# A four-layer fp32 block on one core: split weights kept in place, loads by piece, x turned by the host, two steps moved to ScalarE

## The reference, cut to what matters

```python
def first_block(x, ...):
    x = x + even_layer(x, ...)   # layer 0: chunk attention + mLSTM
    x = x + odd_layer(x, ...)    # layer 1: RG-LRU + gated delta rule
def second_block(x, ...):
    h = _layer_ab(h, ...)        # layer 2: dilated + differential attention
    h = _layer_c(h, ...)         # layer 3: causal attention, 16 heads
    return _rmsnorm(h, final_norm)

def odd_layer(x, ...):
    proj = rmsnorm(x, norm_g) @ w_in
    ...
    qkv = silu(causal_dwconv(concatenate([qd, kd, vd]), conv_d_w))
    q = l2norm(q); k = l2norm(k)
    beta = sigmoid(b_pre); g = -exp(a_log) * softplus(a_pre + dt_bias)
    od = gated_delta_chunkwise(q, k, v, beta, g)   # needs inv(I + strict lower matrix)
    yd = rmsnorm(od, onorm_g) * silu(zd)
    y = concatenate([yc, yd]); return y @ w_out
```

## Time and profile before

| | |
|---|---|
| median of 3 runs | 1970.77 us (1970.48 to 1971.33) |
| the profiled execution | 1970.41 us, its span 1968.6 us |
| PE matmul busy | 1932.7 us, 98% of the span |
| DVE, ACT, POOL busy | 1166.8 (59%), 1005.2 (51%), 172.6 us (9%) |
| chain that ended last | PE 94%, DVE 3%, ACT 1%, issue 1% |
| DMA | 338.44 MB, mean 172 GB/s |

### The profile page before, as it was taken

One profiled execution on the slowest core, in us unless ns is written; L12 is line 12 of the kernel. 1 busy time (PEld: TensorE's weight loads), 2 busy tenths in 40 slices (PEclk: granted clock), 3 DMA queues, 4 the chain that ended last, 5 costly groups with the idle time before them and its releaser, 6 DMA issues.

```text
span 1968.6 us, 28920 instructions
## 1 busy us (share of the span) xinstructions
PE 1932.7 (98%) x11932; PEld 1736.6 (88%) x11932; DVE 1166.8 (59%) x1635; ACT 1005.2 (51%) x1547; POOL 172.6 (9%) x162
## 2 busy tenths in 40 slices
PE   8999999999999999989999999999999999999997
PEld 7988888888899999889899899888889989988886
DVE  5445554555556776877566567655556656654554
ACT  5344445664556645755553344556554344445643
POOL 0000000110003211301001001000000101100110
PEclk9999999999999999999999999999999999999999
DMA  7555455555554443434555654554555554455553
GB/s 266 172 192 171 160 187 193 162 170 192 173 172 130 135 143 130 150 129 168 175 182 191 194 174 157 183 191 157 172 190 173 188 190 158 158 190 166 170 194 128
DMA packets 172851, 338.44 MB, mean 172 GB/s; under 512 B 9536, under 2 KB 9920, under 8 KB 172592
## 3 DMA queue, kind: packets, MB, share of 16 engines
q1 hardware_dynamic: 171632, 332.83, 51.4%
q0 software_dynamic: 944, 3.61, 0.6%
q10 hardware_dynamic: 144, 0.16, 0.0%
HBM read 334.47 MB, written 2.10 MB: 171 GB/s over the span
## 4 chain that ended last, share of the span: by engine, by line
PE 94%; DVE 3%; ACT 1%; issue 1%; DMA 0%; SPq 0%; DVEq 0%; ACTq 0%
PE ACC L680 17%; PE ACC L682 17%; PE ACC L681 17%; PE ACC L687 11%; PE ACC L688 11%; PE ACC L689 11%; DVE WL L1295 1%; DVE S L1525 1%; PE PM L770 1%; PE PM L703 1%; PE PM L785 1%; ACT WH L981 1%; PE PM L823 1%; PE PM L891 1%; PE PM L807 1%
## 5 line engine op out<-in xcount | busy, mean ns | idle before, releaser
L1295 DVE TENSOR_TENSOR WL<-RAW,WH 128x1024 fp32r<-128x1024 f32 x624 | 782.9, 1268 | 623.6 <-ACT WH L981 622.1
L981 ACT ACTIVATE WH<-RAW 128x1024 fp32r<-128x1024 f32 x626 | 652.2, 1054 | 544.8 <-PE ACC L682 303.3
L687 PE MATMUL ACC<-XH,WH 128*128 128x256 f32 x1920 | 554.2, 289 | 3.9 <-DVE WL L1295 3.7
L688 PE MATMUL ACC<-XL,WH 128*128 128x256 f32 x1920 | 545.9, 284 | 0.0
L689 PE MATMUL ACC<-XH,WL 128*128 128x256 f32 x1920 | 545.9, 284 | 0.0
L680 PE MATMUL ACC<-WH,XH 128*128 128x512 f32 x1024 | 406.5, 397 | 0.0
L682 PE MATMUL ACC<-WH,XL 128*128 128x512 f32 x1024 | 399.0, 390 | 0.0
L681 PE MATMUL ACC<-WL,XH 128*128 128x512 f32 x1024 | 398.7, 389 | 0.0
L687 PEld LDWEIGHTS ACC<-XH,WH 128*128 128x128 f32 x1920 | 371.5, 194 | 6.2 <-DVE WL L1295 4.7
L688 PEld LDWEIGHTS ACC<-XL,WH 128*128 128x128 f32 x1920 | 371.5, 193 | 0.9
L689 PEld LDWEIGHTS ACC<-XH,WL 128*128 128x128 f32 x1920 | 371.1, 193 | 0.0
(11 more groups left out here) (328 smaller groups left out, 1646.2 us busy)
## 6 DMA issues: line engine op xcount, KB each, us to landing
RAW<-in_ev_w_in SPq DMA_DIRECT2D x71, 1024.0 KB, 4.9
RAW<-in_w_in_ab SPq DMA_DIRECT2D x64, 1024.0 KB, 5.2
RAW<-in_w_in_c SPq DMA_DIRECT2D x64, 1024.0 KB, 5.2
RAW<-in_od_w_in SPq DMA_DIRECT2D x48, 1024.0 KB, 5.0
RAW<-in_ev_w_out SPq DMA_DIRECT2D x16, 1024.0 KB, 4.9
RAW<-in_od_w_out SPq DMA_DIRECT2D x16, 1024.0 KB, 4.9
RAW<-in_w_out_ab SPq DMA_DIRECT2D x16, 1024.0 KB, 4.9
RAW<-in_w_out_c SPq DMA_DIRECT2D x16, 1024.0 KB, 4.9
```

Source lines behind the costliest of these rows:

```text
L687: e.matmul(o, wh, xh, start=f and g % 2 == 0, stop=False, skip_group_check=True)
L688: e.matmul(o, wh, xl, start=False, stop=False, skip_group_check=True)
L981: e.activation(hi, src, ACT.Copy).then_inc(s_hi)
L1295: e.tensor_tensor(lo, src, hi.bitcast(F32), ALU.subtract).then_inc(s_lo)
```

## The change

- `RAW` becomes eight buffers of one piece, and `WL` lies on the same memory: DVE writes the low half over the weights it reads. `WH` has six buffers, `LOOK` is 5. Each load is one piece (512 KB), and SP issues it when PE has done the products of eight pieces earlier (`s_mm` in place of `s_lo`).
- The host hands over x turned (`xT`, in six parts). SP's first load is a part of it; PE's transposes of layer 0 go, and ACT and DVE make `XH` and `XL` from `Y` between the first eight splits (`x0`). Five matmuls on zeros (`warm`) stand ahead of the first product. x itself, the constants and the rows are loaded later; `squares` move to slots 8 to 11, `rms_a` to 12, `rms_b` to 13.5, and the first evacuation from piece 7 to piece 14.
- `norm_sq` goes from POOL to ACT. The product with `tree` becomes a third memset on POOL and four ACT copies in part 1 of `tri`.
- The gain `onorm` is applied by the scale of `ty`'s evacuation (`og`), and POOL's two products with it go.
- `turn_v` moves to slots 31, 33 and 57, 59; the second half's `level` from 81..87 to 83..89, its `solve` by two slots, `gate_delta` from 82 and later to 85 and later.

```diff
-NRAW = 3
-NHL = 4
-LOOK = 3
+NRAW = 8
+NHL = 6
+LOOK = 5
+WARM = 5
...
+        pieces.extend((j, 4 * r + 2 * h, 2) for r in J.order for h in range(2))
...
-        RAW = [sb(f"RAW{i}", 2048) for i in range(NRAW)]
+        with ExitStack() as first:
+            RAW = [sb(f"RAW{i}", 1024, F32, first) for i in range(NRAW)]
+        WL = [sb(f"WL{i}", 1024, F32R) for i in range(NRAW)]
         WH = [sb(f"WH{i}", 1024, F32R) for i in range(NHL)]
-        WL = [sb(f"WL{i}", 1024, F32R) for i in range(NHL)]
...
+        ENDS = {p: (j,) for j, p in LAST.items()}
+        ENDS[LAST[0] + 7] = ENDS.pop(LAST[0])
...
+            put(-1, "warm")
             for b in range(4):
-                put((-0.5, 0.5, 2.5, 4)[b], "squares", b)
-            put(5, "rms_a", 0)
-            put(6.5, "rms_b", 0, 1)
+                put(8 + b, "squares", b)
+            put(12, "rms_a", 0)
+            put(13.5, "rms_b", 0, 1)
...
-            for half, at in ((0, (19, 22, 28, 29)), (1, (44, 48, 52, 53))):
+            for half, at in ((0, (19, 22, 31, 33)), (1, (44, 48, 57, 59))):
...
-                    (1, (62, 63), (64, 66, 68, 69, 70), tuple(range(71, 81)), (81, 82, 84, 85, 86, 87), (89, 91, 93, 95, 96),
-                     (98, 99, 101))):
+                    (1, (62, 63), (64, 66, 68, 69, 70), tuple(range(71, 81)), (83, 84, 86, 87, 88, 89), (91, 93, 95, 97, 98),
+                     (100, 101, 103))):
...
             def load(p):
...
+                if p >= NRAW:
+                    e.wait_ge(s_mm, p - NRAW + 1)
+                e.dma_start(dst, src).then_inc(s_raw[p % NRAW], 16)
...
+            def warm(_, b):
+                e.wait_ge(s_warm, 1)
+                for _ in range(WARM):
+                    e.matmul(PM[0][:, :], S5[:, 1024:1152], S5[:, 1024:1536], start=True, stop=True)
...
+            def norm_sq(half, _):
+                e.wait_ge(s_silu, 4 * (3 * half + 1) + 4)
+                if half:
+                    e.wait_ge(s_nt, 1)
+                for j in range(4):
+                    for m, slot in enumerate((QD, KD)):
+                        d = e.activation(S[ZD][:, 512 * j + 256 * m:512 * j + 256 * m + 256], feat(slot)[:, 4 * half + j, :], ACT.Square)
+                d.then_inc(s_nsq)
...
+                if part == 1:
+                    e.wait_ge(s_zero, 3 * half + 3)
+                    for c in QUAD:
+                        upper, right = slice(c.start, c.start + 16), slice(c.start + 16, c.stop)
+                        e.activation(eights(AM(half))[upper, :, right], eights(AT)[upper, :, right], ACT.Copy).then_inc(s_am)
...
                     e.memset(TN, 0.0).then_inc(s_zero)
-                    e.tensor_tensor(eights(AM(half)), eights(AT), con("tree").unsqueeze(1).broadcast_to([128, 8, 128]),
-                                    ALU.mult).then_inc(s_am)
+                    e.memset(AM(half), 0.0).then_inc(s_zero)
```

More of the change, by code:

```diff
@@ L125, in job_list, with piece_list @@
     return jobs
-def raw_list(jobs):
-    raws = []
+def piece_list(jobs):
+    pieces = []
     for j, J in enumerate(jobs):
         if J.n < 128:
-            raws.append((j, 0, 16))
+            pieces.append((j, 0, 16))
             continue
-        raws.extend((j, 4 * r, 4) for r in J.order)
+        pieces.extend((j, 4 * r + 2 * h, 2) for r in J.order for h in range(2))
         if J.name == "out" and J.b == 1:
-            b0, b1 = raws[-8:-4], raws[-4:]
-            raws[-8:] = [r for pair in zip(b0, b1) for r in pair]
-    return raws
+            b0, b1 = pieces[-16:-8], pieces[-8:]
+            pieces[-16:] = [p for i in range(0, 8, 2) for p in b0[i:i + 2] + b1[i:i + 2]]
+    return pieces
 def program(nc, I, out):
@@ L594, in load_x, with load @@
                 e.dma_start(X3[:, :, 512 * q:512 * q + 512], x_rows[:, :, 512 * q:512 * q + 512]).then_inc(s_x[q], 16)
-            def weights(n):
-                j, k0, nk = raws[n]
+            def load(p):
+                j, k0, nk = pieces[p]
                 J = jobs[j]
[L599 to L606, removed]
@@ L619, in sync @@
             load(2)
-            again = pieces[F(2, "zs", 0)][0] + NRAW
-            for n in range(NRAW, len(raws)):
-                if n == again:
+            load_xT(2)
+            load(3)
+            load_xT(3)
+            load(4)
+            load(5)
+            load_xT(4)
+            load(6)
+            load(7)
+            load_xT(5)
+            again = F(2, "zs", 0) + NRAW
+            for p in range(NRAW, NP):
+                if p == again:
                     e.wait_ge(s_evD, at_D(2, "k1", 1))
@@ L1260, in subln @@
                     e.activation(ss, ss, ACT.Sqrt, bias=vec("eps"), scale=1.0 / 256).then_inc(s_sln)
-            steps = {"xt": xt, "squares": squares, "root": root, "rms_a": rms_a, "gates1": gates1, "decay": decay, "pT": pT,
+            steps = {"warm": warm, "xt": xt, "squares": squares, "root": root, "rms_a": rms_a, "gates1": gates1, "decay": decay, "pT": pT,
                      "norm_qk": norm_qk, "qkT": qkT, "scores": scores, "mix1": mix1, "pv": pv, "ty": ty, "conv": conv, "decays1": decays1,
-                     "decays2": decays2, "norm_sum": norm_sum, "turn_v": turn_v, "delta_a": delta_a, "tri": tri, "level_x": level_x,
+                     "decays2": decays2, "norm_sq": norm_sq, "norm_sum": norm_sum, "turn_v": turn_v, "delta_a": delta_a, "tri": tri, "level_x": level_x,
                      "solve4": solve4, "onorm": onorm, "gate_lru": gate_lru, "decay_lru": decay_lru, "root_lru": root_lru,
@@ L1794, in evacuate @@
                         e.tensor_tensor(x, x, row2, ALU.mult).then_inc(s_cx)
-                elif J.kind == "zd":
-                    gain = row("onorm").unsqueeze(1).broadcast_to([128, 4, 128])
-                    for t in range(2):
-                        x = tok(ZD)[:, t, 512 * J.b:512 * J.b + 512].rearrange("p (h c) -> p h c", h=4)
-                        e.wait_ge(s_evA, A_AT[j] - 1 + t)
-                        e.tensor_tensor(x, x, gain, ALU.mult).then_inc(s_zd)
                 elif J.kind == "rope":
```

181 lines of the change are left out of this document (92 added, 89 removed).

## The result

The changed kernel took 1958.41 us (median of 4 runs, 1956.38 to 1958.60) against 1970.62 us, a ratio of 0.9935 (95% interval 0.9918 to 0.9952): 12.2 us faster. The forecast was 1957 us, in a range from 1943 to 1965.

What follows compares the result with a forecast made beforehand. PE was taken as the bound (busy 98% of the span), leaving its idle time and low-clock time to gain: -5.8 + 2.5 + 0.5 - 4 + 0.5 - 4.6 - 2.7 = -13.6 of 1970.41 us, so 1957 us, range 1943 to 1965.

Steps and rivals of the forecast that it cites:

- The start: Start of layer 0: first product at 8.75 us, piece 7 at 29.2 in place of 36.24; 5.8 us gained (4.4 to 7.0).
- Loads by piece, low halves in place: Weight loads of 512 KB landing in 3.8 us, and DVE's split written over its source: nothing charged for either.
- rival 3: Weight loads come late, ACT stands at every split and its attention steps delay PE: slower, 1997 us; chance 0.04.
- Squares on ACT: Layer 1's first half, between decays1 and decays2: squares of 2.7 to 3.2 us make PE wait at decays3, +2.5 us.
- The clock's "+0.5": Layer 1, behind the new wait at decays3: a longer stretch at the lower clock, +0.5 us (0 to 1.7).
- The first half's chain: Layer 1: the ACT and DVE chain of conv, delta and tri up to level_x gets shorter, -4 us (-2 to -8.0).
- some 6 us: Layer 1's first half: PE's predicted wait between norm_sum and level_x, until ACT's part 9 of tri is done.
- The low clock behind `level_x`: Layer 1's first half: the clock is low behind PE's wait at level_x, +0.5 us.
- The second half: Layer 1: level_x two pieces later, its wait shrinks from 5.1 to 0.4 us (-4.6), full clock behind it (-2.7).
- 1: Rival: the waits vanish, part 9 of tri is done when PE comes, squares fit ACT's idle time: 1947 us; chance 0.17.
- 2: Rival: ACT becomes the bound of layer 1, with squares at 3.2 us and piece 0 cold: 1966 us; chance 0.10.
- 4: Rival: the start gains nothing as turned x delays the weights, and the chain decides both halves: 1969 us; chance 0.05.

Runs made afterwards that it cites:

- e3: The changed kernel without the five matmuls on zeros (WARM 0 in place of 5): 1957.55 us, ratio 0.9937.
- e11: The changed kernel with all six parts of the turned x loaded ahead of the first piece of weights: 1962.12 us, ratio 0.9961.
- e5: The changed kernel itself, unedited, timed again: 1955.56 us, ratio 0.9933.
- e8: The changed kernel with the first half's squares back on POOL and the second half's on ACT: 1951.81 us, ratio 0.9910.
- e6: The changed kernel with the masked block made by POOL's product again, without the third memset and the four ACT copies: 1958.17 us, ratio 0.9938.
- e7: The changed kernel with turn_v back in slots 28, 29 and 52, 53: 1960.81 us, ratio 0.9954.
- e2: The changed kernel with LOOK 3 and four WH buffers in place of 5 and six: 1958.07 us, ratio 0.9939.
- e4: The kernel before with only the change's later second-half slots and the first half's gate_delta at 85, 87, 89: 1965.58 us, ratio 0.9975.

## Why the prediction was right, point by point

**The start: right in kind, 1.5 us too small** (-5.8 forecast, -7.3 measured at `decays3`, just beyond the upper end of 7.0). Two terms were mis-sized. The DMA moved 383 GB/s from 4 to 6 us, where 253 had been taken from the kernel before, so the first piece's split began at 5.84 and the first product came at 8.21 in place of 8.75, with piece 1 right behind it and not at 11.95. And "the five matmuls on zeros end near 6 us and PE idles until 8.75" failed: they last until the first product (their span ends at 8.45 by the model of ends), and the whole of piece 0 ran at 0.12 us a matmul. e3 puts the clock's part at 1.9 us, and e11 shows that the bytes ahead set the moment. `rms_b` was charged at 0.7, but the lead falls by no more than 0.4 from piece 7 (36.24 - 28.58 = 7.66) to `decays3` (7.29), by which it has been paid. In the earlier trace rows `rms_b` stands just ahead of piece 7 and not behind it, and the 256 KB of x ahead of the first weights are an eighth of x and not a quarter; no term changes by either.

**Loads by piece, low halves in place: nothing, as forecast.** The rows of the page, after and before:

```profile
L1330 DVE TENSOR_TENSOR WL<-RAW,WH 128x1024 fp32r<-128x1024 f32 x624 | 782.9, 1268 | 620.1 <-ACT WH L985 618.3
...
RAW<-in_ev_w_in SPq DMA_DIRECT2D x144, 512.0 KB, 3.5
```

```profile
L1295 DVE TENSOR_TENSOR WL<-RAW,WH 128x1024 fp32r<-128x1024 f32 x624 | 782.9, 1268 | 623.6 <-ACT WH L981 622.1
```

1268 ns for DVE's split in both; 3.5 us to land where 3.8 were taken. The 3.2 us that the prediction worked out from the Trainium skill (page "DMA: Bandwidth & Descriptors", section "Anatomy of one DMA") come from a fit for transfers issued from GpSimd; these loads are SP's. Nothing of rival 3 is to be seen: PE waits for no low half outside the start. No run takes the one-piece loads or the shared memory back by itself; that they cost nothing is read from these rows.

**Squares on ACT: the wait right, the clock too small.** 1.95 us of idle time against 2.5: the squares took 2.55 us, just under the 2.7 to 3.2 charged, and there were 0.4 of slack. The clock's "+0.5" (0 to 1.7) was the mis-sized term: it cost 1.8 in this execution, by the lead's fall from 5.34 us (7.29 - 1.95) to 3.54. In e5's execution the low stretch there is 3.4 us shorter, worth 1.7. e8 puts the whole at 3.75 us by the medians, against e5 on the same chip.

**The first half's chain: right, -4.5 where -4 was forecast.** The lead grows from 3.54 to 8.04 us between the decays and `level_x`, and PE does arrive ahead of part 9 and wait. The "some 6 us" of this wait don't follow from the prediction's own terms: waits of 8.0 us taken away, less the 4 that the chain loses, leave 4, and 4.7 were measured. e6 puts the mask's product at 2.4 us (2.1 forecast), e7 `turn_v` at 3.4 with the clock behind it (2 forecast, 1 to 3 as its bounds), e2 the lookahead at nothing in this half. The two measured parts make 5.8, so they overlap with each other or with the rest. The low clock behind `level_x`, "+0.5", came as -0.4: the lead is 8.41 us at 831.85. The kernel before was at the lower clock there too: its `level_x` took 3.65 us, that of the changed kernel 3.75.

**The second half: -5.6 where -7.3 was forecast.** The lead goes from 8.41 to 14.0. The wait at `level_x` is gone and the clock is up, as said. What the prediction left out is the steps behind: with products at the full clock, `level_y` comes before ACT has evacuated `level_x`, which stands behind three splits (843.22 to 846.06), so 1.1 us of wait is new. With 0.9 at the last `level_x` and 0.6 at the last `level_y` that makes 2.6, where the kernel before had 1.3. That is 1.3 us of wait more; with 5.1 of wait gone and 2.7 for the clock, -6.5 would be due, and 0.9 us are not placed. The step was also charged as if it stood alone: with lookahead three, a wait for low halves stands behind it (2.3 us in e4, 2.8 in e2), so some 1.9 us of what was gained here belong to the lookahead, which the prediction priced in the first half alone. That POOL's product with `onorm` costs nothing here was tested by no run.

**Sum.** -7.3 + 1.95 + 1.8 - 4.5 - 0.4 - 5.6 = -14.05 in the profiled execution, against -13.6; by the medians it is -12.2. The mechanisms were the forecast ones, but that the sum came so near is partly luck: too small a gain at the start and in the chain, too small a loss at the decays and too large a gain in the second half happened to cancel. Of the rivals, 1 failed at `decays3` and at `level_x`, where PE does wait; 2 had the squares' loss right but not the rest; 3 and 4 did not occur.

## What to carry to other kernels

When PE waits for a chain that runs through two other engines, removing one of its waits moves the waiting to the next join; count what the chain itself loses, and put the join later by as many slots as cover it, looking at the step behind the join too. The products that then stand in the place of the wait need their weights split in time, so the lookahead belongs to the same edit (1.9 us here, between e2 and e5). A short job that changes engine must be placed by who waits behind it in that engine's queue: eight squares of 2.55 us in front of a logarithm that PE's next step hangs on cost nearly 4 us, and the same eight in the second half nothing that could be measured. Idle time of TensorE is worth more than its length where the clock falls behind it (1.95 us at `decays3` and 3.75 with what lay behind), and less where PE would have waited at the next join anyway.

## What the runs showed of the hardware

- The stretch at the lower clock behind the decays had different lengths in two executions of the same kernel (granted 0.80 and 0.86 over 25 us, 10 and 7 us), with the same idle times. Single executions here differ by up to 4 us (1954.73 to 1958.73), which blurs edits of that size. Traces with the same granted clock in the same stretch tell them apart: e2 and e3 lie 1.9 and 1.6 us behind e5.
- In e3 the first products ran 0.21 us apart, where those of the changed kernel ran 0.12 apart, and the granted clock of the stretch (8 to 12 us) reads 1.00 all the same. At the very start of these traces the pace of the matmuls tells the clock, and the record doesn't.
- Six taps on DVE took 4.60 us beside a product on POOL and 2.45 beside a memset on POOL (e6 and the changed kernel).
- DVE wrote its result over one of its two sources at 1268 ns a split, the same as into a buffer of its own.
